# One block's search moved behind three others, routing shares in two parts, and an earlier start of the one-hot weave in a two-layer decoder step

## What is computed

```python
def run(xb):
    q = (xb @ w_q).reshape(blk, PEER_HEADS, 2, PEER_QDIM // 2)
    s = jnp.einsum("thpd,pnd->thpn", q, keys).astype(jnp.float32)
    sv, si = lax.top_k(s, PEER_TOPK)
    cand = sv[:, :, 0, :, None] + sv[:, :, 1, None, :]
    cidx = si[:, :, 0, :, None] * N_KEYS + si[:, :, 1, None, :]
    best, pos = lax.top_k(cand.reshape(...), PEER_TOPK)
    eidx = jnp.take_along_axis(cidx.reshape(...), pos, axis=-1)
    g = jax.nn.softmax(best, axis=-1)
    act = jax.nn.gelu(jnp.einsum("thkd,td->thk", u_tab[eidx], xb).astype(jnp.float32))
    return jnp.einsum("thk,thkd->td", (g * act).astype(xb.dtype), v_tab[eidx])
```

## Time and profile before

| | us |
|---|---|
| median of 3 runs | 5103.86 |
| lowest and highest | 5088.18, 5124.47 |
| the profiled execution, its time | 5085.89 |
| its span, first to last instruction | 5084.3 |
| PE busy | 4774.3 (94%) |
| DVE busy | 2933.4 (58%) |
| POOL busy | 1867.7 (37%) |
| ACT busy | 1065.0 (21%) |

### The profile page before, as it was taken

How to read it: one execution, slowest core, us unless ns; L and a number is a source line. 1 busy time by engine, 2 the same in 40 slices (tenths; PEclk the granted TensorE clock), 3 DMA queues, 4 the chain that set the end, 5 groups by cost and what they waited for, 6 DMA issues and landing times.

```text
span 5084.3 us, 84473 instructions
## 1 busy us (share of the span) xinstructions
PE 4774.3 (94%) x25204; PEld 3783.1 (74%) x25204; DVE 2933.4 (58%) x5739; ACT 1065.0 (21%) x2658; POOL 1867.7 (37%) x2649
## 2 busy tenths in 40 slices
PE   7999989888899999999999998998979999999998
PEld 5887777567777777777778877766768777767776
DVE  3653432434589688666636444324345997876665
ACT  1012111310111677000011121112101116760000
POOL 4541330136124344444446313201460343444443
PEclk9999999989999999999999999998899999999999
DMA  7764889689369999999968549895983799999998
GB/s 286 258 232 156 283 272 305 203 314 322 123 242 369 335 361 340 399 409 402 414 250 283 201 155 325 253 315 176 326 314 100 276 367 333 362 334 407 417 404 327
DMA packets 729818, 1519.25 MB, mean 299 GB/s; under 512 B 65297, under 2 KB 406289, under 8 KB 727393
## 3 DMA queue, kind: packets, MB, share of 16 engines
q0 software_dynamic: 256224, 888.06, 46.9%
q1 hardware_dynamic: 473216, 626.61, 36.1%
HBM read 1341.42 MB, written 307.21 MB: 324 GB/s over the span
## 4 chain that ended last, share of the span: by engine, by line
PE 57%; DMA 18%; issue 9%; DVE 7%; SPq 4%; DVEq 3%; POOL 1%; POOLq 1%; ACT 1%; another core or an unknown queue 0%; ACTq 0%
PE PS L1375 18%; DMA xT<-v_rows,arena 10%; PE PS L872 8%; PE PS L760 6%; PE PS L1307 4%; PE PS L999 3%; DVE PS L2065 2%; PE PS L1326 2%; PE PS L1387 2%; PE PS L1331 2%; DMA hT<-v_rows,arena 2%; DMA u_rows<-arena 2%; SPq L526 1%; PE PS L783 1%; PE PS L795 1%
## 5 line engine op out<-in xcount | busy, mean ns | idle before, releaser
L1375 PE MATMUL PS<-hT,ring 128*128 128x288 f32 x4096 | 1014.6, 406 | 0.0
L1432 PE MATMUL PS<-arena,ring 128*128 128x288 f32 x4096 | 993.9, 406 | 0.0
L1432 PEld LDWEIGHTS PS<-arena,ring 128*128 128x128 f32 x4096 | 778.1, 190 | 215.6 <-issue 1.0
L1375 PEld LDWEIGHTS PS<-hT,ring 128*128 128x128 f32 x4096 | 768.5, 190 | 201.6
L2065 DVE SCALAR_TENSOR_TENSOR PS<-xT,arena,PS 128x1024 f32<-128x1024 f32 x374 | 482.2, 1289 | 240.7 <-DMA xT<-v_rows,arena 225.1
L872 PE MATMUL PS<-hT,ring 128*128 128x272 f32 x2304 | 603.4, 408 | 6.3 <-DMA ring<-in_wst 6.3
L739 POOL DMA_INDIRECT xT<-u_rows,arena x410 | 401.1, 978 | 508.0 <-DVE arena L2056 415.4
L599 POOL DMA_DIRECT2D u_rows<-arena x864 | 478.0, 554 | 187.7 <-DVE arena L1583 108.6
L2292 ACT ACTIVATE arena<-PS 128x272 f32<-128x272 f32 (+20 forms) x578 | 221.1, 392 | 1502.3 <-PE PS L872 526.3
L2056 DVE CUSTOM_DVE_ANT_0 xT<-xT,PS 128x1024 f32<-128x1024 f32 x410 | 493.8, 1215 | 38.2 <-DMA xT<-u_rows,arena 35.2
L872 PEld LDWEIGHTS PS<-hT,ring 128*128 128x128 f32 x2304 | 437.6, 197 | 99.2 <-issue 16.8
(11 more groups left out here) (423 smaller groups left out, 5731.5 us busy)
## 6 DMA issues: line engine op xcount, KB each, us to landing
ring<-in_uv SPq DMA_DIRECT2D x512, 512.0 KB
ring<-in_wst SPq DMA_DIRECT2D x296, 512.0 KB
v_rows<-in_uv SPq DMA_DIRECT2D x256, 512.0 KB, 7.0
arena<-in_uv POOLq DMA_DIRECT2D x216, 512.0 KB, 6.1
u_rows<-arena POOLq DMA_DIRECT2D x864, 128.0 KB, 4.8
arena<-in_ck SPq DMA_DIRECT2D x96, 256.0 KB, 5.5
xT<-in_uv POOLq DMA_DIRECT2D x40, 512.0 KB, 6.1
u_rows<-xT POOLq DMA_DIRECT2D x160, 128.0 KB, 5.8
```

The source lines that it names most:

```text
L1375: i = mm(PS[:, 2 + s % 2, 0:TD], ring[:, s, c, :], hD[:, c, :], start=(c == 0), stop=(c == DC - 1))
L1432: i = mm(PS[:, 2 + b, 0:TD], ring[:, s, j, :], WB[:, row, :], start=(row == 0), stop=(row == NK - 1))
```

## The change

The search of block 1 goes behind that of block 4, and behind the signal that the routes of the dense blocks are ready. Only the shares of blocks 2, 3 and 4 are exponentiated and divided at first, between tiles 47 and 48 of the U pass; those of blocks 0 and 1 in the weave, the exponential on ACT at group 8 and the division on DVE at group 12. PE turns the routes behind tile 55 instead of 63, the first group follows tile 58 instead of 65, so 70 groups are in the U pass and 2 behind it (63 and 9 before). Rows up to number 252 instead of 240 are to be done in the U pass.

```diff
-N_EARLY = 112
+N_EARLY = 124
-I_RT, I_OH = 64, 65
+I_RT, I_OH = 56, 58
+G_SHARE = 8
...
-            for n, (p, known) in enumerate(zip(BLOCKS, (0, P, P, P, P))):
-                topk(n, p, known)
+            def shares(h0, h1):
+                g3, sm = GW[:, 16 * h0:16 * h1].rearrange("p (h k) -> p h k", k=16), SM[:, h0:h1]
+                NV.tensor_reduce(sm, g3, AX.X, ALU.add)
+                v.drain()
+                NV.reciprocal(sm, sm)
+                v.drain()
+                tt(g3, g3, bc(sm.unsqueeze(2), [P, h1 - h0, 16]), ALU.mult)
+                v.drain()
+
+            for n in (0, 1, 2, 4):
+                topk(n, BLOCKS[n], P if n else 0)
...
+            shares(16, 34)
...
             v.drain().then_inc(rt_v.sem, 1)
+            topk(3, BLOCKS[3], min(at + 6, P))
+            v.drain().then_inc(tk_v.sem, 1)
...
-            rows(at + 5)
+            rows(at + 1)
...
                 weighted(g, m)
+                if g == G_SHARE + 4:
+                    v.wait_ge(sx_e.sem, sx_e.at(l, 2))
+                    v.nop(nofuse=True)
+                    shares(0, 16)
...
-            dots(0, I_RT - 4)
+            dots(0, I_RT - 8)
...
-            act(GW, GW, ACT.Exp).then_inc(sx_e.sem, 1)
+            act(GW[:, 2 * P:544], GW[:, 2 * P:544], ACT.Exp).then_inc(sx_e.sem, 1)
...
-            dots(I_RT - 4, I_RT)
+            dots(I_RT - 8, I_RT)
...
+                if g == G_SHARE:
+                    s_.wait_ge(tk_v.sem, tk_v.at(l, 2))
+                    s_.nop(nofuse=True)
+                    act(GW[:, 0:2 * P], GW[:, 0:2 * P], ACT.Exp).then_inc(sx_e.sem, 1)
```

More of the change, by code:

```diff
@@ L419, in build @@
     sc_mm, sc_s, sc_us = Sig("key_scores_mm", 9), Sig("key_scores_ready", 9), Sig("key_scores_used", 9)
-    tk_v, sx_e, rt_v = Sig("best_centred", 1), Sig("best_exp", 1), Sig("routes_ready", 1)
+    tk_v, sx_e, rt_v = Sig("best_centred", 2), Sig("best_exp", 2), Sig("routes_ready", 1)
     vn_ld = Sig("v_rows_laid", 16 * NK)
```

## The result

The changed kernel takes 5116.66 us (median of 20 runs, 5107.13 to 5137.84), the kernel before 5104.74 (20 runs, 5088.18 to 5124.47). The ratio is 1.003, with a 95% interval of 1.0019 to 1.0041: slightly slower, by 10 to 21 us. The forecast was 5,107. The profiled execution has a span of 5106.8 us (5084.3 before) at nearly the same mean granted clock (0.968, 0.967 before).

The account below looks back on a forecast made before the run. It took DVE's gathered rows to end each layer: V pass 2.3 us earlier, two more rows 3.9 later, net 1.6 later a layer, 3.2 in all, giving 5,107 us on the median's scale; range 5,073 to 5,144.

Parts of the forecast that it names:

- Search order: U pass before the weave: block 4 searched after block 3, first Exp done at 1624.9, DVE idle 17 us.
- Block 1 searched bare: Before the weave: block 1's search with 6 rows just fits, some 3 us to spare, price 0.
- Rival C: Before group 0: block 1's search overruns its 3 us and PE stands, 8 us a layer; 5,123 us, chance 0.07.
- The weave's own instructions: Weave inside the U pass: 69 intervals of 4.775 us, 16.2 for 27 late one-hots, 2.1 for the rest.
- two-row gaps: Weave: where DVE takes two rows between a weighting and the next one-hots, those come late, 0.60 us each.
- The second Exp: Weave, group 8: the Exp delays ACT's next one-hots 2.3 us; DVE's shares of blocks 0 and 1 cost 0.5.
- DMA in the weave: Weave: traffic rises from 358 to 370 GB/s, costing only more small waits, 1.4 us.
- Rival B: Weave: U rows and tiles capped at 360 GB/s, late rows delay PE; price 33 us, 5,137 us, chance 0.13.
- The groups behind: Between U pass and V pass: seven fewer groups leave 13.6 us of 36.2.
- Rows left: V pass: 257 rows left for DVE instead of 255, 2 x 1.96 = 3.9 us later.
- A layer ends when its rows end: End of layer: V pass start plus rows still to come times 1.96 us; PE's own end a few us earlier.
- Both ways named for being wrong: V pass starting more than 8 us from 2031, or rows ending at another distance from its start than 504 us.

Follow-up runs that it names:

- e1: The changed kernel with every second U row replaced by a 1 KB transfer; span 5095.6 us, weave 350.5 and 352.2 us.
- e8: The changed kernel's search order and two Exps, with weave start and early rows as before and 20 rows filling DVE's wait; 5115.94 us, ratio 1.0026 to the kernel before.
- e3: The changed kernel without the second exponential and the division of the shares of blocks 0 and 1; weave 359.4 and 357.6 us.
- e10: The changed kernel with every second V row replaced by a 1 KB transfer; 5108.54 us once.
- e5: The changed kernel with the first exponential four tiles earlier and 18 rows instead of 6 in block 1's search; 5090.29 us, ratio 0.9987 to the kernel before.
- e4: The changed kernel, same 182 weave rows, but exactly one between a weighting and the next one-hots; 5102.02 us, ratio 1.0003 to the kernel before.
- e7: The changed kernel with 240 rows instead of 252 before the end of the U pass; 5133.44 us, ratio 1.0057 to the kernel before.
- e9: The kernel before with exactly one row between a weighting and the next one-hots, nothing of the change; 5091.47 us, ratio 0.9977.
- e6: The kernel of e5 with exactly one row between a weighting and the next one-hots; 5064.82 us, ratio 0.9937 to the kernel before.
- e2: The changed kernel with U rows fetched from the table of V rows; 5128.79 us once.

## Why the prediction was right, and where its steps failed

The time, 5116.66, lies in the range 5073 to 5144, 10 us above the forecast, and "within 1%, a little slower" is right: of the change's large parts (seven groups, seven intervals, twelve rows) nearly nothing is left. Step by step:

1. *Search order* held. The first shares came 188.9 us into the U pass (forecast: 1624.9 less 1436.0, 188.9), DVE's idle time was 16.5 us for 17.
2. *Block 1 searched bare* held: 229.6 forecast and measured. Rival C falls.
3. *The weave's own instructions* held: 4.78 and 5.30 us intervals, and with the late gathers taken away (e1) 350.5 and 352.2 for 350.6. (Of the 11 two-row gaps before, 10 lie inside the 62 intervals. The table below counts 10 and has 2.4 and 2.7 for the rest instead of 1.8 and 2.1; that moves the sum by 0.6.)
4. *The second Exp* was 2.8 us, and 3.2 in e8: 1.7 for the Exp, for which 2.3 was forecast, and 1.5 for the division of the shares, for which 0.5 was. The whole is nearly right because the two misses have opposite signs. In e3 the weave is 3.6 and 5.9 us shorter, but with 2.4 and 5.2 us fewer waits for rows. In the changed kernel ACT is away from 1709.16 to 1712.19; in layer 0 a fall of the clock behind PE's stand adds 1.66 us, which the prediction didn't have. The Trainium skill, ScalarE: Activation LUTs, "What ACT_TABLE_LOAD costs", adds a drain of 1380 ns to the load of 1283; the rows above show loads of 1.28 us with 0.02 us before the next instruction, as before, and no such drain. By the page the item would be 5.3 us by estimate, and e8 has 3.2.
5. *DMA in the weave* is the step that failed: "I expect only more small waits: 1.4 us". They cost 11.3 to 12.5 (e1), and that moves the weave from 352 to 363. The working averaged: 370 GB/s needed (368 to 375 forecast, 356 measured), 411 seen in the V pass. But a row is asked for only when DVE has used the one before in that buffer, and it takes 7.2 us to land in a crowded weave and 7.3 in an easy one (e10, e5): what counts is when rows are asked for. That DVE's times are set by ACT and PE in the weave, unlike in the V pass, is my reading. Rival B had the mechanism (late rows behind weightings) and nearly the time of the weave (361.8 for 360 GB/s), but its cause, a ceiling, is refuted: 372 and 367 GB/s with the same rows in e4, and landings as quick as elsewhere. The Trainium skill, DMA: Bandwidth & Descriptors, "Where 436 GB/s comes from", has the HBM side bind at about 358 GB/s; 407 to 413 in the V passes of both kernels (2100 to 2500, 4650 to 5000) and 372 in e4's weave are above it.
6. *The groups behind* held: 13.6 forecast, 13.9 and 13.4 measured.
7. *Rows left* failed the other way: two more rows were to cost 3.9 us behind the V pass's start (504.1 in all). They ended 499.8 and 495.8 us after it. 1.96 us a row is right where rows are many (e7), but at 255 to 257 rows PE's 497.8 us stand level with them (e10), and the end is the later of two. "A layer ends when its rows end" was read from layer 0 alone, where the last row came 2.5 us behind PE's end. In layer 1 of the same trace the row ended at 5059.9 and PE at 5060.2, 497.4 and 497.7 us after the V pass's start; the kernel before already showed that PE's end counts as much. This gave back some 4 to 8 of the 11 us.

Both ways named for being wrong came true in the trace: the V pass started 11.3 us from 2031.2 on the scale of before (2042.5), and the rows ended at 499.8, not 504. The total stayed near because the two misses have opposite signs, and that is luck. In a layer: forecast 1.6 later, measured 8.6 and 6.0.

The sum of step 3, without its DMA item and with 3.2 us for the second Exp, can be held against every run (62 or 69 intervals of 4.775 us, 0.60 for each two-row gap, 2.4 or 2.7 for the rest; an estimate, fitted to the first row alone, with the 3.2 from e8):

| kernel | intervals, two-row gaps | sum | weave, layers 0, 1 | U waits |
|---|---|---|---|---|
| before | 62, 10 | 304.5 | 304.5, 304.4 | 5.0, 1.9 |
| e9 | 62, 0 | 298.5 | 298.7, 299.8 | 6.7, 6.6 |
| e8 | 62, 12 | 308.9 | 307.9, 308.1 | 3.8, 2.9 |
| e1 | 69, 27 | 351.6 | 350.5, 352.2 | 0.0, 0.7 |
| e5 | 69, 19 | 346.8 | 347.6, 347.2 | 4.1, 3.7 |
| e7 | 69, 19 | 346.8 | 348.6, 346.6 | 6.1, 3.9 |
| e6 | 69, 0 | 335.4 | 337.8, 338.4 | 10.7, 10.5 |
| e3 (no Exp) | 69, 27 | 348.4 | 359.4, 357.6 | 17.6, 15.8 |
| after | 69, 27 | 351.6 | 363.0, 363.5 | 20.0, 21.0 |
| e2 | 69, 27 | 351.6 | 360.9, 365.6 | 17.3, 21.0 |
| e4 | 69, 0 | 335.4 | 347.5, 353.1 | 22.1, 27.5 |
| e10 | 69, 27 | 351.6 | 364.1, 364.2 | 26.0, 22.4 |

With under 7 us of waits the weave is within 2 us of its sum. With over 15 it is longer than the sum by half to two thirds of the waits. Where waits are few, a further term of more than a us or two has no room.

Where did the expected gain go? The seven groups that leave the stretch behind the U pass gave 22.3 and 24.3 us, as expected. They came back as seven more intervals, late one-hots, the second Exp, and waits for rows. The root of the last is upstream, and e5 shows it: DVE idles 16.5 us for the Exp, and block 1 is searched with 6 rows in it, so that only 70 rows, not 92, are done before the weave. Of these 22, ten go with the weave's earlier start (92 rows in 256.8 us before, one in 2.8, would be 82 in 229.6); the other twelve are those that e5 takes back. 182 rows must then pass through 70 intervals, 2.6 each, against 148 through 63, 2.35 each. Twelve rows back in the search (e5), or twelve asked for later (e7), bring the weave to 347 to 349 either way; but e7 pays for them at the end.

What stays open: where the edge lies. Five rows take 10.0 us in the weave of the changed kernel (5 x 363 / 182), 10.2 in e5 and 10.3 before; a landing of 7.2 and DVE's use of 1.2 leave 1.6, 1.8 and 1.9 us, while single landings go up to 9.2. This estimate says that there was little room in any of them, but not why a few tenths make the waits five times as long. More buffers weren't tried.

## What to carry to other kernels

When work is moved ahead of a signal that others wait for, look at what it carried: the search of block 1 had 24 gathered rows woven into it, and their loss, not the search, was what the next stage paid. A mean rate below a rate seen elsewhere proves no slack if requests are made only as buffers come free; compare the time that the buffers take to go round once with the time from issue to landing. Keep what stands between one engine's result and the next engine's wait the same in every interval (here one row between a weighting and the next one-hots, never two: 0.2% on the kernel before, 0.5% between e5 and e6). Where two engines finish together, price a shift by the later of the two, not by the slope of one.

## What the runs showed of the hardware

- 356 GB/s at a DMA share of 0.97 was no limit: the same tiles and rows went at 372 and 0.98 in a weave that was shorter for another reason (e4), and the V passes had 407 to 413. A gather of 512 KB took 7.2 to 7.4 us from issue to landing (medians) in weaves with 4 and with 26 us of waits (e5, e10).
- ACT's switch to the Exp and back took 3.03 us (two table loads of 1.28 us and an Exp of 0.42). In a round of ACT, DVE and PE of 4.8 us it cost 1.7 us (e8).
- Behind a stand of PE of 2.13 us the granted clock was 0.5 for 3.4 us, and 24 matmuls took 6.67 us instead of 5.01. In e1 it fell likewise behind 2.25 us in layer 1 (0.55 from 4257.6 to 4261.0), but not behind 2.26 in layer 0 (1.00 from 1729.9 to 1733.3). Between the groups behind the U pass, where PE stands before each, it fell in every layer, for 3.4 to 10.2 us.
- The first group came at 229.6 in most profiled layers, but at 231.8 to 232.0 in some (both of e2, one each of e1, e3, e6, e7 and e10); in e9, whose edit lies behind it too, at 256.8 and 259.1. In each of these eight layers, and in no other, the granted clock is at its lower level when the U pass begins. Its first 4.6 us in layer 0 of e2, and the same place of the changed kernel:

```profile
1446.90:1451.50 4.60, 4.60 (x12) 3.31 (x12) 4.13 (x36) 0.00 (x0) 0.00 (x0) 0.50 0.02 4
...
1433.90:1438.60 4.70, 4.70 (x22) 3.70 (x22) 4.33 (x28) 0.48 (x1) 0.00 (x0) 1.00 0.72 304
```

Half the clock, half the matmuls: that is the 2.2 us. In these cases the clock had been down for 9 us before the U pass; why in some executions and not in others isn't shown.
